# A transformer chain in 32-bit floats: weight products with plain 32-bit operands instead of high and low parts

## The reference, cut to what matters

```python
hn = rmsnorm(h, norm_mix[l]);  proj = jnp.einsum('bsd,de->bse', hn, w_in[l])      # 1024 x 10264
y  = sigmoid(gate_fox) * (y_fox @ w_branch_fox) + sigmoid(gate_gdn) * (y_gdn @ w_branch_gdn)
h  = h + y @ w_out
up = causal_dwconv(rmsnorm(h, norm_ffn) @ w_up, ffn_conv_w)                        # 1024 x 5632
h  = h + (silu(u_gate) * u_val) @ w_down                                           # 2816 x 1024
# then 4 times: h = h + mixer(rms_norm(h)); h = h + relu(rms_norm(h) @ w_up_2)**2 @ w_down_2   # 1024 x 4096 x 1024
```

## Time and profile before

| | |
|---|---|
| median of 3 runs | 1794.69 us (1790.66 to 1800.91) |
| span of the profiled execution | 1788.5 us |
| PE (TensorE matmul) busy | 1692.9 us, 95% |
| VectorE busy | 1148.7 us, 64% |
| ScalarE busy | 929.6 us, 52% |
| GpSimd busy | 227.2 us, 13% |
| read from HBM | 268.04 MB, 150 GB/s over the span |

### The profile page before, as it was taken

One profiled execution on the slowest core, in us unless ns is written; L12 is line 12 of the kernel. 1 busy time (PEld: TensorE's weight loads), 2 busy tenths in 40 slices (PEclk: granted clock), 3 DMA queues, 4 the chain that ended last, 5 costly groups with the idle time before them and its releaser, 6 DMA issues.

```text
span 1788.5 us, 26374 instructions
## 1 busy us (share of the span) xinstructions
PE 1692.9 (95%) x9272; PEld 1431.8 (80%) x9272; DVE 1148.7 (64%) x1954; ACT 929.6 (52%) x1502; POOL 227.2 (13%) x301
## 2 busy tenths in 40 slices
PE   7999999999999987999998899998799999799998
PEld 6888988887788865798886698887598888579887
DVE  6666544456687768755566666557755665875665
ACT  5462354554545465654446554447754445565443
POOL 3004520100000005200003400002100000510000
PEclk9989999999999998999999999999899999899999
DMA  8440036636465552356664156654076665245662
GB/s 278 133 134 9 1 99 183 189 121 215 137 197 166 163 181 86 110 185 188 188 187 153 52 183 188 189 162 136 26 236 189 190 190 154 82 124 182 189 188 81
DMA packets 158512, 270.27 MB, mean 151 GB/s; under 512 B 15244, under 2 KB 42331, under 8 KB 158427
## 3 DMA queue, kind: packets, MB, share of 16 engines
q1 hardware_dynamic: 156907, 263.35, 47.5%
q0 software_dynamic: 1504, 5.79, 0.9%
q10 hardware_dynamic: 16, 0.00, 0.0%
HBM read 268.04 MB, written 1.07 MB: 150 GB/s over the span
## 4 chain that ended last, share of the span: by engine, by line
PE 83%; DVE 8%; ACT 4%; issue 2%; POOL 2%; DMA 0%; DVEq 0%; SPq 0%; ACTq 0%; POOLq 0%
PE p_AC L2489 11%; PE p_AC L2491 11%; PE p_AC L2490 11%; PE p_UP L2489 6%; PE p_UP L2491 6%; PE p_UP L2490 6%; PE p_TP L2522 5%; PE p_UP L2522 5%; PE p_TP L2556 3%; PE p_UP L2523 3%; PE p_TP L2523 3%; PE p_AC L1148 1%; ACT t_lg L1514 1%; PE p_UP L1136 1%; PE p_AC L1150 1%
## 5 line engine op out<-in xcount | busy, mean ns | idle before, releaser
L2001 DVE TENSOR_TENSOR t_wl<-t_raw,t_wh 128x1024 fp32r<-128x1024 f32 (+2 forms) x521 | 605.3, 1168 | 468.2 <-ACT t_wh L1406 465.5
L1406 ACT ACTIVATE t_wh<-t_raw 128x1024 fp32r<-128x1024 f32 (+2 forms) x525 | 529.6, 1015 | 574.7 <-PE p_AC L2491 265.8
L2489 PE MATMUL p_AC<-t_wh,t_uTh 128*128 128x512 f32 (+1 forms) x612 | 240.3, 393 | 9.5 <-DVE t_uTl L2182 3.9
L2491 PE MATMUL p_AC<-t_wh,t_uTl 128*128 128x512 f32 (+1 forms) x612 | 238.7, 390 | 0.0
L2490 PE MATMUL p_AC<-t_wl,t_uTh 128*128 128x512 f32 (+1 forms) x612 | 238.4, 390 | 0.0
L2489 PE MATMUL p_UP<-t_wh,t_hT 128*128 128x512 f32 (+2 forms) x544 | 214.6, 394 | 4.4 <-DVE t_hT L2046 4.4
L2491 PE MATMUL p_UP<-t_wh,t_hT 128*128 128x512 f32 (+2 forms) x544 | 210.9, 388 | 0.0
L2490 PE MATMUL p_UP<-t_wl,t_hT 128*128 128x512 f32 (+2 forms) x544 | 210.6, 387 | 0.0
L2522 PE MATMUL p_TP<-t_hT,t_wh 128*128 128x512 f32 x384 | 144.4, 399 | 0.0
L2522 PE MATMUL p_UP<-t_hT,t_wh 128*128 128x512 f32 x384 | 144.0, 398 | 0.0
L2489 PEld LDWEIGHTS p_AC<-t_wh,t_uTh 128*128 128x128 f32 x612 | 115.3, 188 | 34.6 <-DVE t_uTl L2182 7.9
(11 more groups left out here) (347 smaller groups left out, 2819.6 us busy)
## 6 DMA issues: line engine op xcount, KB each, us to landing
t_raw<-in_w_up SPq DMA_DIRECT2D x128, 512.0 KB, 4.1
t_raw<-in_w_down SPq DMA_DIRECT2D x128, 512.0 KB, 4.1
t_raw<-in_w_in SPq DMA_DIRECT2D x72, 512.0 KB, 3.7
t_raw<-in_w_up SPq DMA_DIRECT2D x88, 256.0 KB, 4.1
t_raw<-in_a_w_in SPq DMA_DIRECT2D x24, 512.0 KB, 3.7
t_raw<-in_w_down SPq DMA_DIRECT2D x44, 256.0 KB, 3.2
t_raw<-in_a_w_out SPq DMA_DIRECT2D x16, 512.0 KB, 3.7
t_raw<-in_b_w_in SPq DMA_DIRECT2D x12, 512.0 KB, 3.8
```

Of the source, the lines that this page charges most:

```text
L1406: A_(wh[:, c % SPL, 0:size(c)], raw[:, c % RAW, 0:size(c)], ACT.Copy).then_inc(high_done, 1)
L2001: V.tensor_tensor(wl[:, c % SPL, 0:n], raw[:, c % RAW, 0:n], wh[:, c % SPL, 0:n].bitcast(F32), ALU.subtract).then_inc(split_done, 1)
L2489: M(outs[t], a_hi, w_hi[:, k, :], start=first and k == 0, stop=False)
L2491: ins = M(outs[t], a_lo, w_hi[:, k, :], start=False, stop=last and k == ch.nk - 1)
```

## The change

All high and low parts go. Weight products read the loaded chunk itself and activations in one 32-bit copy, with one call of matmul each. `raw` has 16 chunks, `wh` and `wl` are gone. A load waits until TensorE has finished the chunk 16 before it; TensorE waits for the arrival of a chunk itself. Feed-forwards are Python loops instead of `Fori` on all engines. The up products of the squared feed-forwards all have 256 columns, in the bank pair TP for even slices after the first and UP for odd ones. ReLU and square are done in halves, with no sum of two halves of a result. ScalarE's `high`, `highs`, VectorE's `rest`, `rests`, `low_half`, the `u_low` and `output_low` steps and GpSimd's `pool_rest` are deleted from all places. Waits for a low part become waits for the single copy (`t_split` to `t_high`, `ul_done` to `u_done`, `ol_done` to `oh_done`, `o_done` to `fh_done`).

```diff
-RAW, SPL = 8, 4
+RAW = 16
-        wh = sb("wh", [P, SPL, CHUNK], F32R)
-        wl = sb("wl", [P, SPL, CHUNK], F32R)
-        hT = sb("hT", [P, KD, 2, S], F32R)
-        uTh = sb("uTh", [P, 4, S], F32R)
-        uTl = sb("uTl", [P, 4, S], F32R)
+        hT = sb("hT", [P, KD, S])
+        uT = sb("uT", [P, 2, 4, S])
...
+        def up_bank(j, half):
+            return acc(2 + half) if j == 0 else (up if j % 2 else tpb)(half)
+        def up_end(c0, j):
+            return c0 + (8 * j if j else 4)
...
@@ SyncE
-            def load(c, j=None, it=0):
+            def load(c):
                 if c >= RAW:
-                    sp.wait_ge(split_done, c - RAW + 1 + (8 * it if j is not None else 0))
+                    sp.wait_ge(spl_free, c - RAW + 1)
...
@@ ScalarE
-            def high(c, it=None):
...
-                A_(wh[:, c % SPL, 0:size(c)], raw[:, c % RAW, 0:size(c)], ACT.Copy).then_inc(high_done, 1)
...
+                for j in range(n):
+                    act.wait_ge(spl_free, up_end(c0, j))
+                    for half in range(2):
+                        if j:
+                            act.wait_ge(u_done, ub + 2 * j - 1 + half)
+                        A_(hid[:, half * COLS:(half + 1) * COLS], up_bank(j, half), ACT.Relu).then_inc(hid_done, 1)
...
@@ VectorE
-            def rest(c, it=None):
...
-                V.tensor_tensor(wl[:, c % SPL, 0:n], raw[:, c % RAW, 0:n], wh[:, c % SPL, 0:n].bitcast(F32),
-                                ALU.subtract).then_inc(split_done, 1)
...
+                for j in range(n):
+                    conv(j)
+                    dve.wait_ge(gate_done, b + j + 1)
+                    V.tensor_tensor(uT[:, j % 2, 0:2, :].rearrange("p k s -> p (k s)"), slot(0, 512),
+                                    slot(0, 512, 512), ALU.mult).then_inc(u_done, 1)
...
@@ TensorE
+            def weights(c):
+                pe.wait_ge(raw_in(c), arrive[c])
+                return raw_view(c)
...
-                        M(outs[t], a_hi, w_hi[:, k, :], start=first and k == 0, stop=False)
-                        M(outs[t], a_hi, w_lo[:, k, :], start=False, stop=False)
-                        ins = M(outs[t], a_lo, w_hi[:, k, :], start=False, stop=last and k == ch.nk - 1)
+                        ins = M(outs[t], lh[:, k0 + k, t * P:(t + 1) * P], w[:, k, :],
+                                start=first and k == 0, stop=last and k == chunks[c].nk - 1)
...
-                        M(out_, w_hi[:, k, cols], a_hi, start=k0 + k == 0 and m % 2 == 0, stop=False)
-                        M(out_, w_hi[:, k, cols], a_lo, start=False, stop=False)
-                        ins = M(out_, w_lo[:, k, cols], a_hi, start=False, stop=k0 + k == KD - 1 and m % 2 == 1)
+                        ins = M(out_, w[:, k, m * P:(m + 1) * P], hT[:, k0 + k, :],
+                                start=k0 + k == 0 and m % 2 == 0, stop=k0 + k == KD - 1 and m % 2 == 1)
...
-            def use_wide(c, it, k0):
...
-                with pe.Fori(2, n - 1) as j:
-                    up_mm(c0 + 4, j)
-                    pe.wait_ge(ul_done, j + b)
-                    dn_mm(c0 + 8, j, False, False)
+                for j in range(2, n - 1):
+                    up_mm(c0 + 8 * j - 4)
+                    dn_mm(c0 + 8 * j, j - 1)
                     transpose_hidden(j)
```

More of the change, by code:

```diff
@@ L1368, in _ @@
                     _, c0, f, n = item
[L1369 to L1377, removed]
+                    for c in range(c0, c0 + 8 * n):
+                        load(c)
             rows_out = out[0].rearrange("(t p) d -> p t d", p=P)
@@ L1395, in link @@
                 act.wait_ge(sem("act_chain"), chain[0])
-            def high(c, it=None):
[L1399 to L1405, removed]
-                A_(wh[:, c % SPL, 0:size(c)], raw[:, c % RAW, 0:size(c)], ACT.Copy).then_inc(high_done, 1)
             def ahead(it):
                 if it < len(items):
[L1410 to L1418, removed]
+                    if it in stage_of and stage_of[it] not in whole:
+                        high_half(stage_of[it], 0)
+                    if it - 1 in stage_of and items[it - 1][0] == "block":
+                        high_half(stage_of[it - 1], 1)
+                        if it - 1 != after_final:
+                            sum_squares(stage_of[it - 1])
                     if it - 1 == after_final:
@@ L1421, in ahead, with read_block @@
                         square_rows(rms_index(t_mix[0]))
[L1423 to L1429, removed]
+            def read_block(it, dst, w, scale=None, func=ACT.Copy, square=None, stages=True):
+                if stages:
                     ahead(it + 1)
@@ L2097, in att_core @@
                         half_norm_dve(dve, V, n, 1)
-                    if n % 3 == 1 and i == 3:
-                        rests(blocks["out"][0], 3, 4)
                     if i < PAIRS:
@@ L2469, in _, with features_high, use @@
             att_wait = [None]
-            def use(c, it, outs, lh, ll, k0, first, last):
-                pe.wait_ge(split_done, c + 1 if it is None else it * 8 + (c + 1 - 8))
-                ch = chunks[c]
-                w_hi = wh[:, c % SPL, 0:size(c)].rearrange("p (k n) -> p k n", k=ch.nk)
-                w_lo = wl[:, c % SPL, 0:size(c)].rearrange("p (k n) -> p k n", k=ch.nk)
-                for k in range(ch.nk):
-                    if second_half[0] is not None and lh is hTh and (k0 + k) % 2 == 0:
-                        pe.wait_ge(t_split, second_half[0] + (k0 + k) // 2 + 1)
-                        if k0 + k == KD - 2:
-                            second_half[0] = None
+            def weights(c):
+                pe.wait_ge(raw_in(c), arrive[c])
+                return raw_view(c)
+            def features_high(lh, k):
+                if second_half[0] is not None and lh is hT and k % 2 == 0:
+                    pe.wait_ge(t_high, second_half[0] + k // 2 + 1)
+                    if k == KD - 2:
+                        second_half[0] = None
+            def use(c, outs, lh, k0, first, last):
+                w = weights(c)
+                for k in range(chunks[c].nk):
+                    features_high(lh, k0 + k)
                     if att_wait[0] is not None:
@@ L2543, in block_mm @@
                 for i, ch in enumerate(cs_):
[L2544 removed]
+                    use(c0 + i, [bank(g, t, w) for t in range(NT)], lh, k0, i == 0, i == len(cs_) - 1)
                     k0 += ch.nk
@@ L2547, in block_mm @@
                         stage_half(n, 1)
-                    if k0 == KD // 2 and lh is hTh and tail is not None:
+                    if k0 == KD // 2 and lh is hT and tail is not None:
                         stage_half(tail, 0)
```

565 lines of the change are left out of this document (106 added, 459 removed).

## The result

The changed kernel takes 2087.07 us (median of 3 runs, 2087.03 to 2088.34) against 1794.69: ratio 1.1635, 95% interval 1.1595 to 1.1676, so 16.4% slower. The forecast was 2098, with a range of 2055 to 2145. The span of the profiled execution is 2085.3 us, 296.8 more than before. One execution in eleven of the kernel before (2226.39 us) and one in five of e4 (2794.26 us) ran at a mean granted clock near 0.72 instead of 0.97 to 0.99, and these two count in no ratio; the second is also the profiled one of e4, whose trace is not read here.

The account below looks back on a forecast made before the run. TensorE, busy 1692.9 of 1788.5 us, was taken to bound the kernel. Adding 341 us for products and subtracting 37 us of idle time gave 2092.5, with 6.2 to the median 2098 us; range 2055 to 2145.

Parts of the forecast that it names:

- The cost of a product: On TensorE, 512-column products go from 0.681 to 0.861 us, 256-column ones to 0.435; 341 us added in all.
- What is given back: Idle time of TensorE that disappears once the splitting goes: 37 us in all, bounds 15 and 75.
- start: First product waits 2.68 us for the low half of the activations; the high half is ready sooner, returning 1.7 us.
- its last down product: Gated feed-forward: of a 3.86 us wait, 2.4 us go through a shorter convolution chain and longer products above it.
- query norms and attention cores together: Three attention starts waiting on the query norm return 10 us, the four attention cores 11 us.
- elsewhere, idle time: Transitions and short waits elsewhere in the kernel return 9 us, bounds 0 and 20.
- attention cores: I take a third of VectorE's: Four attention cores: VectorE loses 32 us of splitting, of which 11 us come back; bounds 0 and 32.
- 1 (idle time shrinks by 80): Attention cores shrink with VectorE's load and 80 of TensorE's 96 idle us go: 2056 us; chance 0.12.
- 2 (14 ns in plain records too): The 14 ns beside the columns belong to 512-column weight products, whatever the operand type: 49 us more, 2147; chance 0.12.
- 3: Plain weight loads come out from under the matmul: about 3040 us; chance 0.03, shared with a lower granted clock.
- 4 (one record per product): A plain product is one record, not two, costing 0.4305 us at 512 columns: 1258 us; chance 0.02.
- 5: The change does not do what it says, or waits and cost cancel; chance of the same time 0.01.

Follow-up runs that it names:

- e4: The changed kernel with each 512-column product in four matmuls of 128 columns: 2143.51 us, ratio 1.1941.
- e2: The kernel before with all its splitting kept, but each weight product one matmul with plain 32-bit operands: 2106.97 us, ratio 1.1737.
- e7: The kernel before with its three float32r matmuls per product reordered, so that neighbouring matmuls write different PSUM banks: 1795.16 us, ratio 1.0005.
- e6: The changed kernel with GpSimd's power in the query and key norms replaced by a multiplication of the same shape: 2085.29 us, ratio 1.1627.
- e5: The kernel before with its splitting kept, but one float32r matmul per weight product, high by high: 1343.68 us, ratio 0.7493.

## Why the prediction was right, point by point

**The bound.** "What one product costs TensorE afterwards" was the question, and e2 answers it alone: plain products by themselves cost 312 us, more than the 292 of the whole change; the deletions then return 20.

**The cost of a product.** Predicted 0.861 and 0.435 us, measured 0.858 and 0.432. The four nanoseconds beside the columns, taken from records of 128 and 256 columns, are 2 to 3 in the dense stretches. By the measured spacings the sum is 1440 x 0.177 + 768 x 0.079 + 256 x 0.072 = 255 + 61 + 18 = 334 us, where 341 were predicted. (The upper bound of that sum is 390 by its own terms, 341 + 2 x 10 ns x 2464, and not 395.) The spacing of 131 ns for 512-column matmuls, which the Trainium skill's page "TensorE: Matmul & The Clock Gate" gives in its section "Back-to-back issue gap", is not seen in any run here: 227 ns in e7 as in the kernel before, and 429 ns for a plain record.

**What is given back.** 334 - 297 = 37 us, the number predicted, but its parts moved, and that they add up to the same is luck:

| part | predicted | measured |
|---|---|---|
| start (2.68 us of waiting, now 2.16) | 1.7 | 0.5 |
| first down product of the gated feed-forward (3.25, now none) | 3.1 | 3.2 |
| its last down product (3.86, now 1.43) | 2.4 | 2.4 |
| query norms and attention cores together | 21 | 14 |
| elsewhere, idle time | 9 | 9 |

The idle time of TensorE fell by 29 us in all, so 8 of the 37 are not in it, and the 96 idle us were not all that there was to give back. The mean granted clock rose from 0.983 to 0.988: time at the lower level, 1.2 GHz, fell from 2 x 0.017 x 1788.5 = 61 us to 2 x 0.012 x 2085.3 = 50. Work there takes twice as long (1.42 us for 0.73 under e6), which gives some 5 us as an estimate. The prediction had no term for this. The last 3 are not attributed. The waits at the start and at the last down product in the changed kernel, from the timeline of TensorE:

```profile
9.98 4.61 PE L2128 MATMUL p_UP<-t_raw,t_hT 128*128 128x512 f32 x5 [2.16 <-ACT t_hT L1383]
733.93 2.41 PE L2128 MATMUL p_AC<-t_raw,t_uT 128*128 128x512 f32 x5 [1.43 <-DVE t_uT L1908]
```

**The step that was off** is "attention cores: I take a third of VectorE's". In the four attention stretches, cut at the same instructions of TensorE, its idle time went from 14.0, 14.7, 14.6 and 14.0 us to 10.7, 11.9, 10.2 and 10.0, together from 57 to 43. The first and the third, in the kernel before, in e2 and in the changed kernel (columns as in the earlier trace rows):

```profile
686.50:751.90 65.40, 51.42 (x304) 38.07 (x303) 53.61 (x166) 39.48 (x107) 32.28 (x36) 0.90 0.26 80
1227.00:1293.10 66.10, 51.55 (x318) 40.46 (x318) 52.59 (x176) 54.38 (x143) 17.95 (x15) 0.92 0.16 52
```

```profile
798.50:867.40 68.90, 56.92 (x267) 31.16 (x266) 52.97 (x163) 38.79 (x106) 32.23 (x36) 0.93 0.25 77
1442.20:1510.20 68.00, 54.84 (x292) 36.89 (x294) 52.55 (x175) 54.35 (x143) 18.08 (x15) 0.92 0.15 47
```

```profile
785.00:852.80 67.80, 57.06 (x268) 31.06 (x267) 40.33 (x146) 29.21 (x95) 27.68 (x34) 0.90 0.23 70
1425.00:1489.30 64.30, 54.12 (x294) 36.67 (x294) 42.61 (x158) 48.17 (x134) 16.90 (x15) 0.92 0.24 74
```

In e2, where all the splitting stays, the four come to 48 us. So 9 of the 14 us come with the longer products alone, and the deletions add 5.

Of the 14, the starts gave the 10 that were predicted: the waits on the first query norm fell from 10.6 us in three places to 0.6. (The prediction read 4.22 us for each of the three; the second of them was 2.1, but nearly all of each went.) So the cores gave 4, where 11 were taken. The second wait on the norm grew, from 7.7 us in three places to 10.7. In the first core, before (now 3.77, under e6):

```profile
707.17 1.07 PE L2556 MATMUL p_AC<-t_ident,t_A 128*128 128x128 f32 x8 [1.75 <-DVE t_A L838]
```

The chain behind it has no splitting in it. Pieces of the chain of the changed kernel in that core, in order of time (start, us, what):

```profile
796.93 1.16 ACT t_A L1350 x2
798.19 1.23 DVE t_sm L809
799.76 2.89 POOL t_sm L1749
802.65 0.42 POOL t_A L1773
803.07 1.13 POOL t_A L1774
```

TensorE's result is read by ScalarE, summed by VectorE, taken to a power by GpSimd for 2.89 us, and then GpSimd's masks follow. The busy share of VectorE in the core (37.53 of 44 us) had suggested that any load taken off it would count; its splitting did not stand on this chain. e6 shows that no single piece holds the end: beside the power stand VectorE's top-k and mask of nearly the same length. How the remaining idle time divides between these and softmax is not shown by any run.

**The offset to the median.** I carried 6.2 us from the span to the median. After the change the median is 1.8 us above the span of the profiled run: the profiled execution of before was one of the quicker ones of a spread of 10 us, the one of after was typical of a spread of 1.3. So of the 11 us between forecast and median, 7 are on the span (the cost of a product, 341 against 334) and 4 are this offset.

**The rivals.** 1 (idle time shrinks by 80): no, by 29. 2 (14 ns in plain records too): no, 2 to 3. 3: no, starts 429 ns apart in the changed kernel itself, and e4. 4 (one record per product): excluded by the counts. 5: did not arise.

## What to carry to other kernels

When one engine is 95% busy, count what a change issues on it before counting what it takes off the others: here 1268 us of work taken off VectorE and ScalarE were worth some 20 us, and 0.177 us added to each of 1440 products cost 255. Read the price of an operation that the trace lacks from narrower ones of the same kind, by start-to-start spacing and records per call. And where an engine waits in a core of short steps, follow the chain before crediting lighter load on a busy engine: a chain across engines doesn't shorten when work that is not on it leaves one of them, and taking out a piece that is on it gains only what no other work of the same length covers.

## What the runs showed of the hardware

- A matmul with plain 32-bit operands is two records, each taking two cycles a column at 2.4 GHz and 2 to 3 ns besides (0.429 us for 512 columns, 0.216 for 256); one with float32r operands takes one cycle a column and 14 ns besides (0.227 us for 512). Three float32r matmuls therefore take 0.79 of the time of one plain one. The 14 ns are the same whatever bank the neighbouring matmuls write (e7).
- The loads of the kernel, which never needed over 190 GB/s, ran at 324 GB/s over 30 us in e5 when the chunks were consumed faster, with the DMA engines busy for 0.99 of that stretch.
- Weight loads of plain operands last 190 ns in the records and start as often as the records do, 111 ns apart in the delta rule; four times as many of them, each under a record of 128 columns, cost 6.5 ns for each load and record added (e4).
